# Layer 0's long feed-forward: who computes the low parts of the up weights, VectorE or GpSimd

## What is computed

```python
def conv_ffn(h, w_up, conv_w, conv_b, w_down):
    a = h @ w_up                     # [tokens, 1024] @ [1024, 5632]
    a = depthwise convolution of width 3 along the tokens + conv_b
    gate, val = jnp.split(a, 2, axis=-1)
    return (jax.nn.silu(gate) * val) @ w_down
```

## Time and profile before

| | |
|---|---|
| median of 3 runs | 1774.03 us (1773.12 to 1774.28) |
| the profiled execution, its own time | 1770.33 us |
| its span in the trace | 1768.5 us |
| TensorE busy | 1692.3 us, 96% of the span |
| VectorE, ScalarE, GpSimd busy | 1236.0, 867.4, 201.6 us |
| low parts of weights by VectorE | 356 pieces, 387.6 us |
| low parts of weights by GpSimd | 56 pieces, 136.6 us |
| chain of work that ended last | TensorE 81%, VectorE 14%, ScalarE 3% |

### The profile page before, as it was taken

The page is one execution under the profiler, slowest core; times in us unless marked ns, Lnnn a source line. Parts: engine busy times, 40 slices in busy tenths (PEclk is TensorE's granted clock), DMA queues, the critical chain, the costliest instruction groups (busy, mean ns, idle before and its releaser), DMA issues.

```text
span 1768.5 us, 29212 instructions
## 1 busy us (share of the span) xinstructions
PE 1692.3 (96%) x12118; PEld 1535.7 (87%) x12118; DVE 1236.0 (70%) x2077; ACT 867.4 (49%) x1295; POOL 201.6 (11%) x126
## 2 busy tenths in 40 slices
PE   6999999999999999999899999999999898899999
PEld 6999888898999999998867888788887787699999
DVE  2377479777777886567755798876878668558864
ACT  4422555537555665445666344323432445556653
POOL 5301550000000110000000111101110100041100
PEclk9999999999999999999999999999999899999999
DMA  6553545445354544421101334354335312035544
GB/s 272 217 208 148 212 150 211 183 176 194 140 184 175 185 179 159 165 107 49 49 24 49 120 119 166 132 178 152 139 139 188 128 72 95 2 137 187 181 166 141
DMA packets 41108, 259.75 MB, mean 147 GB/s; under 512 B 4368, under 2 KB 7568, under 8 KB 14480
## 3 DMA queue, kind: packets, MB, share of 16 engines
q1 hardware_dynamic: 40976, 257.88, 39.7%
HBM read 256.82 MB, written 1.05 MB: 146 GB/s over the span
## 4 chain that ended last, share of the span: by engine, by line
PE 81%; DVE 14%; ACT 3%; issue 1%; DMA 0%; POOL 0%; SPq 0%; DVEq 0%; ACTq 0%
PE acc_psum L197 23%; PE acc_psum L198 22%; PE acc_psum L199 22%; PE acc_psum L2430 3%; DVE w_low_sb L163 2%; PE acc_psum L2383 2%; PE acc_psum L1029 2%; PE acc_psum L2409 2%; PE acc_psum L238 1%; DVE mod_products L292 1%; DVE ring_sb L292 1%; PE acc_psum L373 1%; DVE norm_sq_sb L676 1%; DVE u_filtered L1939 1%; DVE norm_rt_sb L1676 0%
## 5 line engine op out<-in xcount | busy, mean ns | idle before, releaser
L197 PE MATMUL acc_psum<-h_high_sb,w_high_sb 128*128 128x256 f32 (+1 forms) x2176 | 667.2, 307 | 10.7 <-DVE h_low_sb L442 4.2
L198 PE MATMUL acc_psum<-h_low_sb,w_high_sb 128*128 128x256 f32 (+1 forms) x2176 | 659.8, 303 | 0.0
L199 PE MATMUL acc_psum<-h_high_sb,w_low_sb 128*128 128x256 f32 (+1 forms) x2176 | 659.8, 303 | 0.0
L152 ACT ACTIVATE w_high_sb<-ring_sb 128x1024 fp32r<-128x1024 f32 (+2 forms) x412 | 386.7, 988 | 404.7 <-PE acc_psum L199 287.4
L163 DVE TENSOR_TENSOR w_low_sb<-ring_sb,w_high_sb 128x1024 fp32r<-128x1024 f32 (+1 forms) x356 | 387.6, 1131 | 85.8 <-ACT w_high_sb L152 75.5
L197 PEld LDWEIGHTS acc_psum<-h_high_sb,w_high_sb 128*128 128x128 f32 x2176 | 413.9, 190 | 38.1 <-issue 14.2
L198 PEld LDWEIGHTS acc_psum<-h_low_sb,w_high_sb 128*128 128x128 f32 x2176 | 414.1, 190 | 17.6 <-issue 0.5
L199 PEld LDWEIGHTS acc_psum<-h_high_sb,w_low_sb 128*128 128x128 f32 x2176 | 413.7, 190 | 16.8
L163 POOL TENSOR_TENSOR w_low_sb<-ring_sb,w_high_sb 128x1024 fp32r<-128x1024 f32 x56 | 136.6, 2463 | 743.0 <-ACT w_high_sb L152 743.0
L1939 DVE SCALAR_TENSOR_TENSOR u_filtered<-acc_psum,par_sb,u_filtered 128x255 f32<-128x255 f32 (+2 forms) x264 | 150.8, 571 | 75.2 <-ACT u_filtered L2076 58.3
L197 PE MATMUL acc_psum<-u_high,w_high_sb 128*128 128x256 f32 (+1 forms) x528 | 170.3, 322 | 9.1 <-DVE w_low_sb L163 9.0
(11 more groups left out here) (303 smaller groups left out, 1995.7 us busy)
## 6 DMA issues: line engine op xcount, KB each, us to landing
ring_sb<-in_w_in SPq DMA_DIRECT2D x68, 1024.0 KB, 6.7
ring_sb<-in_w_up SPq DMA_DIRECT2D x66, 1024.0 KB, 4.8
ring_sb<-in_w_down SPq DMA_DIRECT2D x48, 704.0 KB, 4.1
ring_sb<-in_w_ada SPq DMA_DIRECT2D x24, 1024.0 KB, 4.8
ring_sb<-in_w_ada_rows SPq DMA_DIRECT2D x24, 1024.0 KB, 4.8
ring_sb<-in_w_out SPq DMA_DIRECT2D x12, 1024.0 KB, 4.8
ring_sb<-in_w_br_hg SPq DMA_DIRECT2D x4, 1024.0 KB, 6.9
ring_sb<-in_w_br_ml SPq DMA_DIRECT2D x4, 1024.0 KB, 4.9
```

The costliest lines, as they stand in the source:

```text
L152: self.nc.scalar.activation(self.high[:, g % 2, piece], self.ring[:, c % RING, piece], ACT.Copy)\
L197: nc.tensor.matmul(out, sh, mh, start=start, stop=False)
L198: nc.tensor.matmul(out, sh, ml, start=False, stop=False)
L199: return nc.tensor.matmul(out, sl, mh, start=False, stop=stop)
```

## The change

It names GpSimd for units 1 to 10 of `up` in both halves of layer 0, and VectorE for their units 0, and it puts a call of `split_low` into GpSimd's list in `up`, ahead of `u_low`:

```diff
@@ build @@
             if i < LAYERS - 1:
                 for half in range(2):
-                    add("w_up_2", range(up0 + FFH * half, up0 + FFH * (half + 1)), "dve", "pool", ROW_RIDES[f"up{half}"])
+                    add("w_up_2", range(up0 + FFH * half, up0 + FFH * (half + 1)), "pool", "dve", ROW_RIDES[f"up{half}"])
                     add("w_down_2", range(down0 + half, down0 + 2 * DT, 2), "dve", "dve", ROW_RIDES[f"down{half}"])
@@ up @@
         @block.gpsimd
         def _(pool):
             for n in range(n_units):
+                core.split_low(pool, g0 + n + 1, "pool")
 
                 pool.wait_ge(*hi.at(n + 1))
                 nc.gpsimd.tensor_tensor(ul[:, n, :], tmp[:, 2 * (n % 2), :], uh[:, n, :].bitcast(F32), ALU.subtract)\
```

## The result

| | before | changed |
|---|---|---|
| median, us (runs) | 1774.15 (4) | 1793.42 (4) |
| lowest and highest, us | 1773.12, 1777.07 | 1786.39, 1798.66 |
| ratio of the changed kernel to the one before | | 1.0109, 95% interval 1.0092 to 1.0127 |
| the profiled execution, us | 1770.33 | 1795.09 (span 1793.3) |

The change costs 19.3 us, 1.1%. The forecast was 1794.1 us, 20.1 above the kernel before.

The account below looks back on a forecast made before the run. TensorE was taken to bound the kernel, with VectorE off the path in both up stages. Terms of 16.2 + 1.6 + 2.3 = 20.1 us took the median from 1774.0 to 1794.1 us; range 1783 to 1800.

Parts of the forecast that it names:

- what the relief is worth: Both up stages: taking 47 us of work from VectorE gives 0, except one wait of 0.19 before unit 1.
- A unit with dots, 1.8: Nine up units: u_low and dots take turns, GpSimd's first piece comes late, 1.8 us lost each, 16.2 in all.
- Second pieces, 0.8 in units 1 and 6: Half 0: a dot falls between GpSimd's two pieces, so TensorE waits 0.8 us more in each unit, 1.6 together.
- Units without dots, 0: Up units without dots: GpSimd's low parts come just in time, nothing lost, units stay at 11.15 us.
- The 0.14 to spare: Up unit without dots: TensorE could start at T + 10.81 against a limit of T + 10.95, T being ScalarE's first tap.
- Harmless: the convolution behind it has time: Unit with dots: the fourth dot ends at T + 10.3 in place of 9.0, at no cost.
- the forecast's own signs of being wrong: Up stages: TensorE's stretches stay full, the nine waits are not 1 to 2.5 us, or units without dots wait too.
- The norm, 2.3: Norm ahead of unit 1, half 0: GpSimd's pieces hold VectorE's `low` at line 442; unit 1 starts 2.3 us later, bounds 0 to 3.0.
- The waits of 3.49 unchanged: Ends of the up stages, first `down` unit: TensorE's waits for VectorE, 3.49 and about 3.4 us, stay as they were.
- the rival of the faster side: Stage ends: VectorE's relief shortens both waits, at most to nothing, 6.9 us less, 1767.1; chance 0.03.
- GpSimd does not keep its turn: Rival claimed the opposite: the first piece follows u_low at once, 0.7 lost in nine units, norm 3.0, 1783.3 us; chance 0.10.
- The exclusion holds in all the places named: Rival claimed no exclusion there: units with dots lose nothing, the norm is not held, 1774 us; chance 0.06.

Follow-up runs that it names:

- 20 pieces moved and no new waits: Against the kernel before: half 1's up-stage low parts on GpSimd, that of unit n+2 ahead of u_low of unit n; 1773.24 us, ratio 1.0001.
- the moved dots: Kernel before with the dots of down unit 0 moved to unit 2 in each half; 1763.61 us, ratio 0.9944.
- the one with unit 1 alone: Kernel before with unit 1's low parts in half 0 on GpSimd, and unit 0's on GpSimd in half 1 only; 1776.06 us, ratio 1.0011.
- its partner with short dots: Changed kernel with each dot cut from 1024 to 64 columns, part of the computation left out; 1764.58 us, ratio 0.9953 to the kernel before.

## Why the prediction was right, point by point

**What bounds the kernel, and what the relief is worth.** Right. The kernels with 20 pieces moved and no new waits (1.0001) and with the moved dots on top (0.9936 beside 0.9944) show no worth of VectorE's relief in these stages, to within some 3 us.

**A unit with dots, 1.8.** Right in mechanism; the size was 1.6. In half 1, four units lost 1.55 to 1.62. Of the steps, `u_low` ready at T + 6.96 was exact. It ended at T + 8.99 (9.1 forecast), the fourth dot at T + 10.04 (10.3), and TensorE started at T + 12.40 (12.8). Held instructions end about 0.1 earlier than the sum of their own durations: the dot took 1.05 from `u_low`'s end in place of 1.21. The forecast could have had this from its own rows, where a held dot's end minus the other's end is known.

**Second pieces, 0.8 in units 1 and 6.** Too large. The waits are there, but 0.22 each. Four waits for a first piece of half 0 and its two for a second, TensorE of the changed kernel:

```profile
1042.18 0.47 PE L197 MATMUL acc_psum<-h_high_sb,w_high_sb 128*128 128x512 f32 x1 [0.71 <-POOL w_low_sb L163]
1045.42 0.50 PE L197 MATMUL acc_psum<-h_high_sb,w_high_sb 128*128 128x512 f32 x1 [0.22 <-POOL w_low_sb L163]
...
1055.01 0.50 PE L197 MATMUL acc_psum<-h_high_sb,w_high_sb 128*128 128x512 f32 x1 [0.95 <-POOL w_low_sb L163]
1067.06 0.47 PE L197 MATMUL acc_psum<-h_high_sb,w_high_sb 128*128 128x512 f32 x1 [0.58 <-POOL w_low_sb L163]
...
1103.95 0.47 PE L197 MATMUL acc_psum<-h_high_sb,w_high_sb 128*128 128x512 f32 x1 [1.60 <-POOL w_low_sb L163]
1107.21 0.50 PE L197 MATMUL acc_psum<-h_high_sb,w_high_sb 128*128 128x512 f32 x1 [0.22 <-POOL w_low_sb L163]
```

In unit 1 the first piece was also earlier than summed: the table load put the dots so late that `u_low` met the first of them and not the third. The units behind units 1 and 3 lost 1.43 and 0.83. Unit 3 itself had begun late, behind the wait of 0.95, so its end and the limit for the next low part moved back by about 1.2.

**Units without dots, 0.** Right for half 1. Wrong for one: the unit behind unit 2 of half 0 lost 1.27 (the wait of 0.95 above). The 0.14 to spare was counted from an undisturbed ScalarE, but unit 2 followed unit 1, whose last two dots were held. GpSimd and VectorE:

```profile
1039.71 3.40 DVE L292 CUSTOM_DVE_ANT_0 ring_sb<-ring_sb,cond_rows,par_sb 128x1024 f32<-128x1024 f32 x1
...
1043.04 3.41 DVE L292 CUSTOM_DVE_ANT_0 ring_sb<-ring_sb,cond_rows,par_sb 128x1024 f32<-128x1024 f32 x1
...
1038.66 6.71 POOL L163 TENSOR_TENSOR w_low_sb<-ring_sb,w_high_sb 128x1024 fp32r<-128x1024 f32 x2
1051.33 1.30 POOL L2113 TENSOR_TENSOR u_low<-u_filtered,u_high 128x512 fp32r<-128x512 f32 x1 [5.96 <-ACT u_high L2105]
```

The convolution behind them started at 1046.38, the silu waited for it, and the `u_low` in unit 2 (1051.33, T here 1041.51) came at T + 9.8 in place of T + 6.96. "Harmless: the convolution behind it has time" is the step that failed, in this one unit, where two dots were held for 2.2 each.

Together half 0 lost 9.15 for 10.6. By the forecast's own signs of being wrong (nine waits of 1 to 2.5, none in units without dots) three places speak against it: two of the nine waits were 0.71 and 0.58, and one unit without dots waited 0.95. The other seven were 1.28 to 1.60, none as long as 1.8.

**The norm, 2.3.** By its own terms the sum was 2.4 (2.6 less 0.19). The hold was right: the second `low` lasted 2.19, as forecast with a wait for GpSimd's second piece, and the chain's last `low` came 2.15 later (forecast: 2.6) against the same chain before. Alone it cost 1.8. What had no term is the fall of the clock, 2.2 more in the changed kernel.

**The waits of 3.49 unchanged.** Right in size (7.0 us in two). What they cost was misread: the rival of the faster side priced both at 6.9, and taking them away gave 10.

**The rivals.** GpSimd does not keep its turn: in the units with dots a dot got in between `u_low` and the piece (1248.23 above). The exclusion holds in all the places named. *Faster* did not happen through VectorE's relief, as its 2.67 us of idle time ahead of the last convolution said. The Trainium skill's Perfetto Trace Analysis, section Optimizing Scalar/DVE Operations, which would offload to GpSimd where VectorE is saturated, came out as it warns: offloading to GpSimd did not help, and TensorE waited 12.4 us for GpSimd's low parts. One tile in each half given to GpSimd where TensorE did wait for VectorE may have gained 3 to 4 us, which is not clear of no change.

**The sum** was 20.1; the stretches show 19.5 and the medians 19.3. That it is so near is in part luck: the units were summed 2.2 too high (the nine lost 14.2 for 17.8, the one without dots 1.3 for 0) and the norm's hold 0.5, and the clock, 2.2, was not in it. In the profiles themselves 5.3 us more lie outside the stretches, which the medians do not show.

## What to carry to other kernels

Before work is moved from VectorE to GpSimd, write down for one unit when each of the two starts which instruction, and count that instructions of the kinds seen here, which read two SBUF operands, run one after the other, in turns; the cost falls on whichever of the two is waited for next. Place the GpSimd work early in the unit, beside VectorE work that has time, and look for rides of long side work directly behind a stage's last unit: moving those gained 10 us here, where no use of GpSimd gained anything clear of noise. A busy share of 70 or 80% is no reason to relieve an engine, a wait for it is.

## What the hardware showed that was not expected

**The two engines take turns by whole instructions.** In the rows of these kernels, a dot, a product or a `low` that started while an instruction of GpSimd ran was stretched by the rest of it, and the other way round; with work waiting on both sides they alternate: 1.21 to 2.31, 3.09 or 3.41 for a dot, 0.48 to 2.19 for line 442, a pair of pieces from 4.77 to 6.71. Convolutions, which read PSUM and one buffer, were not stretched: those over 510 columns took 0.75 each in the mean, in the kernel before and in the changed one. The Trainium skill's Perfetto Trace Analysis, section Optimizing Scalar/DVE Operations, tells of a 2-port VectorE operation that holds GpSimd's port as an exclusive lock; these rows show GpSimd holding VectorE just so.

**A short wait can cost more than itself.** Busy time of the kernel before from 1142.0 to 1153.3 us, with the wait of 3.49 in it (engines, then granted clock, DMA share, GB/s):

```profile
1142.00:1153.30 11.30, 7.81 (x28) 6.31 (x28) 11.30 (x20) 1.47 (x2) 0.00 (x0) 0.85 0.45 136
```

and its matmuls behind the wait:

```profile
1146.50 0.39 PE L198 MATMUL acc_psum<-u_low,w_high_sb 128*128 128x512 f32 x1
...
1147.51 0.63 PE L198 MATMUL acc_psum<-u_low,w_high_sb 128*128 128x512 f32 x1
1147.94 0.63 PE L199 MATMUL acc_psum<-u_high,w_low_sb 128*128 128x512 f32 x1
...
1150.61 0.39 PE L197 MATMUL acc_psum<-u_high,w_high_sb 128*128 128x512 f32 x1
```

From about 1146.9 to 1150.2 they follow each other by 0.43 in place of 0.23: TensorE runs at its lower level, 1.2 GHz. The ten spacings from 1146.73 to 1150.61 take 3.88 in place of 2.3, 1.6 more, and from the start of the last matmul ahead of the wait (1141.61) to the second one behind it (1145.82) 3.75 more pass than without it. So the wait cost some 5.4, which is what the stretch gave back when the dots were moved. It is not the same each time: in the changed kernel and in the one with unit 1 alone, the same wait of 3.5 at the first stage end is followed by a granted clock of 0.66 for ten us, and the stretch behind the stage took 78.2 in place of 77.0.

The clock fell behind the norm's hold in the changed kernel too. Windows of 10 us, both from 4.07 behind the second root on, changed kernel first, then the kernel in which only unit 1 is GpSimd's:

```profile
1020.00:1030.00 10.00, 8.46 (x47) 8.26 (x48) 6.81 (x13) 3.06 (x7) 2.09 (x1) 0.66 0.30 105
```

```profile
1016.73:1026.73 10.00, 8.46 (x57) 7.80 (x58) 8.21 (x15) 5.32 (x9) 2.09 (x1) 1.00 0.27 105
```

TensorE's waits ahead are alike in both (1.36 and 1.54; 1.34 and 1.54), yet the clock fell to 0.66 in the one and stayed at 1.00 in the other, with ten matmuls fewer in the same time. It fell in the changed kernel and in its partner with short dots (25.6 and 25.5 us for the stretch), and stayed in the two that took 23.4 us. What decides between them stays open. In the changed kernel's units the waits of 1.3 to 1.6 were not followed by such a fall: the granted clock was 1.00 in each of them.
